# Attention's last stage on Trainium2: the output projection's chunks spread over the query tiles, and the last two done by channel

## The reference, cut to what matters

```
def diff_attend(q, k, v, lam):
    s = jnp.einsum('bqhcd,bkhcd->bhcqk', q, k).astype(jnp.float32) * (DIFF_DH ** -0.5)
    p = jax.nn.softmax(s, axis=-1)
    a = (p[:, :, 0] - lam * p[:, :, 1]).astype(v.dtype)
    return jnp.einsum('bhqk,bkhe->bqhe', a, v)
...
    def finish(o):
        o = rms_norm(o, sub_g) * (1.0 - lam_init)
        return o.reshape(o.shape[0], o.shape[1], D_MODEL) @ w_o
```

## Time and profile before

| | us |
|---|---|
| three runs: lowest, median, highest | 2600.32, 2601.14, 2603.65 |
| the profiled execution | 2600.41 |
| its span in the profile | 2598.6 |
| the last attention iteration, first scores to the first unit behind it | 2130.76 to 2175.78 |

### The profile page before, as it was taken

How to read it: one execution, slowest core, us unless ns; L and a number is a source line. 1 busy time by engine, 2 the same in 40 slices (tenths; PEclk the granted TensorE clock), 3 DMA queues, 4 the chain that set the end, 5 groups by cost and what they waited for, 6 DMA issues and landing times.

```text
span 2598.6 us, 40617 instructions
## 1 busy us (share of the span) xinstructions
PE 2510.0 (97%) x14679; PEld 2223.1 (86%) x14679; DVE 1597.2 (61%) x2500; ACT 873.8 (34%) x1358; POOL 438.2 (17%) x524
## 2 busy tenths in 40 slices
PE   6999999999899999999999999999899998999999
PEld 6888888888788888888889999999789987788887
DVE  6788667224678867883484756574777774433332
ACT  1333223222533312332242433243455553322221
POOL 2022111001212212110100000001477751000000
PEclk6999999999899999999999999999999998999999
DMA  6355543221145544452111222122110111233332
GB/s 222 110 149 162 145 122 105 65 75 42 30 134 150 166 132 129 139 152 69 44 57 57 81 59 79 49 81 65 49 49 24 48 33 49 73 100 94 95 101 87
DMA packets 363902, 238.77 MB, mean 92 GB/s; under 512 B 7633, under 2 KB 362546, under 8 KB 363826
## 3 DMA queue, kind: packets, MB, share of 16 engines
q1 hardware_dynamic: 361984, 237.01, 31.0%
q10 hardware_dynamic: 1842, 0.77, 0.1%
HBM read 235.65 MB, written 2.10 MB: 91 GB/s over the span
## 4 chain that ended last, share of the span: by engine, by line
PE 89%; DVE 5%; ACT 2%; issue 2%; POOL 1%; DMA 0%; SPq 0%; ACTq 0%; DVEq 0%; POOLq 0%
PE pu L1228 62%; PE pu L1376 11%; PE pv L1514 5%; PE pu L1236 3%; DVE h_lo L2075 1%; PE pu L1532 1%; PE pv L1542 1%; PE pu L1551 1%; DVE xn L2067 1%; POOL sqa L632 1%; PE pv L1304 1%; PE pu L1640 1%; PE pu L1487 1%; DVE w_lo L1762 0%; DVE mx L2174 0%
## 5 line engine op out<-in xcount | busy, mean ns | idle before, releaser
L1228 PE MATMUL pu<-h_hi,w_hi 128*128 128x512 f32 x1776 | 508.3, 350 | 2.2 <-DVE w_lo L1762 1.8
L1228 PE MATMUL pu<-h_hi,w_lo 128*128 128x512 f32 x1776 | 506.8, 350 | 0.0
L1228 PE MATMUL pu<-h_lo,w_hi 128*128 128x512 f32 x1776 | 506.1, 349 | 0.0
L1762 DVE TENSOR_TENSOR w_lo<-w_raw,w_hi 128x1024 fp32r<-128x1024 f32 (+3 forms) x228 | 310.6, 1363 | 242.2 <-ACT w_hi L755 234.5
L755 ACT ACTIVATE w_hi<-w_raw 128x1024 fp32r<-128x1024 f32 (+3 forms) x228 | 247.6, 1087 | 573.1 <-PE pu L1228 510.7
L1779 DVE SCALAR_TENSOR_TENSOR ada_acc<-ada_raw,cs,ada_acc 128x384 f32<-128x384 f32 x588 | 337.3, 615 | 10.8 <-DVE ada_acc L1779 1.8
L1228 PEld LDWEIGHTS pu<-h_hi,w_hi 128*128 128x128 f32 x1776 | 285.4, 189 | 49.0 <-DVE w_lo L1762 2.2
L1228 PEld LDWEIGHTS pu<-h_hi,w_lo 128*128 128x128 f32 x1776 | 285.5, 189 | 45.1
L1228 PEld LDWEIGHTS pu<-h_lo,w_hi 128*128 128x128 f32 x1776 | 284.5, 188 | 44.3
L1990 DVE SCALAR_TENSOR_TENSOR xT<-pu,gate,xT 128x512 f32 (+3 forms) x136 | 81.3, 633 | 333.7 <-PE pu L1228 330.5
L684 POOL TENSOR_TENSOR ada_acc<-ada_acc,ada_parts 128x768 f32<-128x768 f32 x84 | 142.3, 1694 | 706.7 <-ACT ada_parts L762 666.4
(11 more groups left out here) (266 smaller groups left out, 4539.8 us busy)
## 6 DMA issues: line engine op xcount, KB each, us to landing
w_raw<-in_ffn_w_in SPq DMA_DIRECT2D x138, 512.0 KB, 3.9
ada_raw<-in_ada_w SPq DMA_DIRECT2D x84, 768.0 KB, 4.7
w_raw<-in_ffn_w_out SPq DMA_DIRECT2D x48, 704.0 KB, 4.7
w_raw<-in_ffn_w_in SPq DMA_DIRECT2D x76, 256.0 KB, 3.0
w_raw<-in_diff_w_qkv SPq DMA_DIRECT2D x24, 512.0 KB, 5.4
first_h<-in_ada_w SPq DMA_DIRECT2D x4, 1536.0 KB, 19.6
w_raw<-in_ffn_w_out SPq DMA_DIRECT2D x16, 384.0 KB, 3.4
w_raw<-in_ffn_w_out SPq DMA_DIRECT2D x16, 320.0 KB, 3.1
```

The costliest lines, as they stand in the source:

```text
L1228: last = pe.matmul(banks(ch, s_), w[:, j, :], r[:, SEG[s_]], start=(j == 0 and i == 0), stop=(j == k - 1 and i == 2))
L1762: dve.tensor_tensor(w_lo[:, ch, 0:k * P], w_raw[:, ch, 0:k * P], w_hi[:, ch, 0:k * P].bitcast(F32), ALU.subtract).then_inc(split_ready[ch], 1)
```

## The change

In the last iteration the chunks 2, 3 and 4 move into the tile loop, each behind the transposes of a tile, and DVE's `out_lo(2)` to `out_lo(4)` with them, each behind `weights_lo` and ahead of `combine`. Chunk 5 takes the place that chunk 2 had. Head 7 is squared straight from the accumulator `pu[:, 0]`, ahead of the copy to `oT`; DVE's norm of head 7 gets a wait for that copy. Behind the loop PE does channel 0 of chunk 6, the sums and the spread of head 7, channel 0 of chunk 7, and then channel 1 of both chunks.

```
--- before.py
+++ after.py
@@ -1143,6 +1143,9 @@
                             square_act(0, t)
                 if not do_a:
                     out_hi(HEADS - 2)
+                    act.wait_ge(pv_done, HEADS)
+                    act.wait_ge(ors_done, HEADS)
+                    act.activation(ob[:], pu[:, 0, :], ACT.Square).then_inc(osq_ready, 1)
                 if do_b:
                     act.wait_ge(pv_done, g + 1)
                     act.activation(oT[:, bass.ds(g, 1), :].rearrange("p o q -> p (o q)"), pu[:, 0, :],
@@ -1205,7 +1208,6 @@
                 attn_act(h, True, True, True)
             attn_act(HEADS - 1, True, True, True)
             attn_act(HEADS, False, True, True)
-            out_square(HEADS - 1)
             out_hi(HEADS - 1)
             for m in range(OUT_PAIRS - 1):
                 for ch in range(2):
@@ -1581,14 +1583,14 @@
                                      start=True, stop=True)
                 last.then_inc(ors_done, 1)
 
-            def out_chunk(j):
+            def out_chunk(j, chs=(0, 1)):
 
                 if j == 0:
                     pe.wait_ge(qkv_out, TT * HEADS)
                     for ch in range(2):
                         pe.wait_ge(split_ready[ch], PAIR_WO + 2)
                 pe.wait_ge(on_split, j + 1)
-                for ch in range(2):
+                for ch in chs:
                     last = chunk(ch, j, DC, h_hi[:, j], h_lo[:, j], NL, wo_banks)
                     if j == HEADS - 1:
                         last.then_inc(unit_done[ch], 1)
@@ -1611,10 +1613,12 @@
                         out_chunk(1)
                     if do_b and 1 <= s <= QT:
                         turn_weights(g, s - 1)
+                    if not do_a and 1 <= s < QT:
+                        out_chunk(s + 1)
                 if do_a:
                     project(h, TT - 1, DC // 2, DC)
                 else:
-                    out_chunk(2)
+                    out_chunk(QT + 1)
                     out_spread(h - 2)
                 if do_b:
                     values(g)
@@ -1742,12 +1746,12 @@
                 attn_pe(h, True, True, True)
             attn_pe(HEADS, True, False, True)
 
-            out_chunk(3)
+            out_chunk(HEADS - 2, (0,))
             out_sums(HEADS - 1)
-            out_chunk(4)
             out_spread(HEADS - 1)
-            for j in range(5, HEADS):
-                out_chunk(j)
+            out_chunk(HEADS - 1, (0,))
+            for j in (HEADS - 2, HEADS - 1):
+                out_chunk(j, (1,))
             for m in range(1, OUT_PAIRS - 1):
                 for ch in range(2):
                     unit(ch, PAIR_WO + m, DC, lambda j: h_hi[:, j], lambda j: h_lo[:, j], NL)
@@ -2234,9 +2238,11 @@
                         row_max(step, g, s)
                     if not do_a and s == QT:
                         out_var(h - 2)
-                        out_lo(2)
+                        out_lo(QT + 1)
                     if do_b and 1 <= s <= QT:
                         weights_lo(g, s - 1)
+                    if not do_a and 1 <= s < QT:
+                        out_lo(s + 1)
                     if do_b and s < QT:
                         combine(step, g, s)
                 if isinstance(h, int) and h == HEADS - 1:
@@ -2356,9 +2362,9 @@
                 attn_dve(h, True, True, True)
             attn_dve(HEADS - 1, True, True, True)
             attn_dve(HEADS, False, True, True)
-            for j in range(3, HEADS - 1):
-                out_lo(j)
+            out_lo(HEADS - 2)
             out_var(HEADS - 1)
+            dve.wait_ge(oT_ready, HEADS + 1)
             out_norm(HEADS - 1)
             out_lo(HEADS - 1)
             for m in range(OUT_PAIRS - 1):
```

## The result

| | before | changed |
|---|---|---|
| median of 9 runs each, us | 2602.33 (2600.32 to 2606.95) | 2608.58 (2605.16 to 2612.97) |
| ratio, 95% interval | | 1.0025 (1.0017 to 1.0034) |
| first scores of the last iteration to `values`, us | 29.88 | 37.24 |
| `values` to the first unit, us | 15.14 | 15.04 |
| the first unit's 96 matmuls in the chain, us | 23.66 | 22.81 |

The kernel became slower by 0.25% by the ratio, 6.25 us by the medians. The forecast was slower by 0.15%, with a range to 2608.5; the measured median lies 0.08 us above it. The upper two rows of the table come from the runs, the lower three from one profile of each. The profiled execution of the change took 2612.97 us, the longest of its nine, and that of before took 2600.41, so a difference between the two profiles need not be that between the medians.

The account below looks back on a forecast made before the run. TensorE is busy for 97% of the span, but waits bound the last iteration's tiles. Terms +5.5 up to `values`, -0.5 behind, -1.0 in the first unit give +4.0 on 2600.41; plus 0.7 for the median: 2605.1 us, range 2600.5 to 2608.5.

Parts of the forecast that it names:

- The wait: Tile loop: each chunk waits for DVE's `out_lo` behind `weights_lo` and delays the scores; three chunks, +7.7 us.
- the 1.0 us of refund within the tiles: Tile loop: the high clock returns for a tile's end, speeding transposes and part of the third chunk; 1.0 us off.
- Its price of 2.56 us for a chunk: Tile loop: assumed cost of one chunk at the low clock, counted three times for +7.7 us.
- Chunk 5 at the high clock: In chunk 2's old place: chunk 5 follows a long busy stretch and runs at the high clock; 1.2 us off.
- Behind `values`: From `values` to the first unit: fewer chunks but new waits, 0.2 to 1.0 us shorter; taken as -0.5.
- The bound of v + 14.9: Behind `values`: latest start of the first unit, counted from the start v of `values`, against 15.14 before.
- The first unit: First unit after the stage: the low clock ends at about its start, giving back 0 to 1.7 us; taken as -1.0.
- The starting point: Whole kernel: profiled 2600.41 us, with 0.7 us added for the median of the runs shown.
- My second rival: Tiles to first unit: chunks stay at 1.2 GHz, the clock gives nothing back; +7.4, 2608.5 us; chance 0.20.
- The fourth rival: Tile loop: the rest comes early enough, so the chunk hides, 0.1 us per tile; -2.4, 2598.7 us; chance 0.06.

Follow-up runs that it names:

- e1: The changed kernel with DVE's `out_lo(s + 1)` moved ahead of the maxima of tile s; ratio to before 0.9995.
- e4: The kernel before with only DVE's rests moved into the tiles, behind `weights_lo`, PE's chunks where they were; ratio to before 1.0001.
- e11: The changed kernel run once more, unaltered; ratio to before 1.0027.
- e5: e1 with chunks 2 and 3 in tiles 1 and 2, none from last transposes to head 6's spread, 4 and 5 halved behind `values`; ratio to before 0.9992.
- e10: e5 with zero-matrix filler matmuls where PE waits, including 3 behind the sums and 3 behind the last transposes; ratio to before 0.9980.
- e6: The kernel before with zero-matrix filler matmuls where PE waits for exponentials in the tiles; ratio to before 0.9988.

## Why the prediction was right and where it was wrong

**The wait: right.** The chunk stands behind `weights_lo` and the rest on DVE, starts when the idle time is over, and pushes the scores by its whole length. The transposes of the last tile came 7.0 us later after the first scores (32.10 against 25.08); the forecast for that point was 7.7 less 1.0. e1 undoes the wait and the loss goes; e4 keeps DVE's part without PE's wait and there is no loss. In the prediction's terms 0.7 of the 1.0 us of refund within the tiles came. Its price of 2.56 us for a chunk was a piece of the chain; from its first matmul to the next work a chunk at the low clock takes 2.71 us (2157.04 to 2159.75 before). Three of those are 8.1 us, and by that price 1.1 came off.

**Chunk 5 at the high clock: wrong.** This is the step that failed. It took 1.2 us off for a chunk at the high clock, and the chunk ran at the low one, 2.71 us, as long as chunk 2 in its place before. The reason that I gave, a long busy stretch before it, was met: PE had been busy for 5.45 us without a pause when chunk 5 began. But the clock stayed at 0.50 through chunk 4, the sums, the transposes and chunk 5, and rose only in the spread: `values` ran at the high clock. The spread took 1.26 us (2170.73 to 2171.99), where it took 0.89 before. The forecast for `values` was 5.5 us later, and 7.4 was measured; of the 1.9 between them, 1.2 is chunk 5, 0.4 the spread and 0.3 the tiles. Why the clock came back within 4.2 us of full work in rows 8 (1868.96 to 1873.15) and here only after 8.2 (2162.57 to 2170.73) is not shown.

**Behind `values`: mis-sized.** The waits came as worked out (1.34 us ahead of the spread, 2.30 ahead of chunk 7), and the square from PSUM took 0.60 where 0.64 was assumed. I took 0.5 us off; the stage became shorter by 0.1, since chunk 7 and what follows ran at the low clock: the end at v + 15.0 and not v + 14.6. The bound of v + 14.9 in the prediction is 0.2 more than its terms add up to (10.8 + 1.3 + 0.17 + 2.41 = 14.7), so its low-clock case was undersized as well: the three matmuls took 1.7 us with their drain (2182.92 to 2184.60), and chunk 7 began at v + 10.9.

**The first unit: near, but the forecast ended there.** 0.85 us came back in it (23.66 to 22.81), against 1.0 assumed. Even so the change has 1.4 us more from the start of the first unit to the end, 2611.2 - 2187.03 = 424.2 against 2598.6 - 2175.78 = 422.8, and e11 has the same 424.2. So 2.2 us were lost behind the first unit, where the prediction has no term. The profiles show where: in the last 33 matmuls of 128x256 ahead of the long block that fills the rest of the span. Windows from the first of them to that block, columns as in rows 2, first in the changed kernel and then in the kernel before:

```profile
2243.85:2250.84 6.99, 6.99 (x33) 6.79 (x34) 2.57 (x4) 3.54 (x5) 0.00 (x0) 0.55 0.07 19
```

```profile
2233.72:2238.14 4.42, 4.11 (x30) 3.70 (x31) 1.71 (x2) 3.08 (x5) 0.00 (x0) 1.00 0.00 0
```

They take 6.99 us after the change and 4.42 before it, and at the lower clock, though nothing in them was changed. From the first unit to them the change is 1.1 us shorter (56.82 against 57.94), and from the long block to the end both have 360.4 or 360.5. Why the clock is low there, some 60 us behind the stage of the change, is not shown.

**The starting point.** I added 0.7 us for the median of three runs; over nine runs the median of before is 1.2 us higher still. The other 2.3 of the 3.5 us by which the median lies above the forecast one are the change's. By the profiles the terms above miss more than that: 1.9 up to `values`, 0.4 behind it, 2.3 from the first unit on, 4.6 in all. The profiles give the change +8.6 us from the first scores on, the medians +6.25; what makes up the 2.4 between them is not shown. My second rival, in which the clock gives nothing back, has 2608.5, all but the measured median, and that is in part luck: its +7.4 was added to a starting point 1.2 us too low. Its mechanism is not what happened: the clock did come back within the tiles (0.67 and 0.73) and in the first unit. What failed to pay was the refund on chunk 5 and that behind `values`.

**The fourth rival**, the chunk hides if the rest comes early enough, is not what the change does, but e1 shows it to be what the change could have done: tiles of 5.97 us, at a clock of 1.00. Yet it wins nothing by itself, because the three chunks were free where they stood, behind `values`, under the steps of head 7's norm. e5 fills both: from the first scores to the first unit it has 43.1 us, where before has 45.0 and e1 45.1, though its total time is not shown to be below before's. e10, with filler besides, has 41.5.

## What to carry to other kernels

Work that is moved into an engine's idle time has to be ready when that time begins; look in the list of the engine that makes its input, not only at the length of the gap. Before moving work out of a stage, see which chain it was covering there. Where TensorE waits inside a short loop, look at its granted clock as well as at the gap: e6 gained 3.1 us (0.12%) with filler alone, and two thirds of the change's loss up to `values` went with the clock.

## What the runs showed of the hardware

The combination on DVE, which reads two tensors from SBUF, takes 1.91 us in place of 1.02 while POOL makes a 128x512 rest of 1.51 to 1.58 us beside it. The Trainium skill ("SBUF — State Buffer", "SBUF: two separate sides") says that VectorE and GpSimd share a pair of ports that one of them holds for a whole instruction, which VectorE needs with two SBUF inputs. The trace agrees in the main: in both pairs of rows above the profile shows the two at once, and the combination ends 0.8 us after POOL's instruction. Had it begun only when POOL's ended, that would be the 1.02 us that it takes alone; the 0.2 between them is not explained.

The pattern of the clock in the last iteration repeats over two profiles of the change, with the same 0.67, 0.73 and 0.52 and the same length up to `values` within 0.01 us, although the iteration starts 1.4 us apart in them.

A stretch of full work does not always bring the high clock at once: in the change PE worked without a pause from 2162.57 on, and the granted clock was 0.50 until the spread at 2170.73.
